# A new order of ScalarE's and GpSimd's steps in three feed-forward blocks, and rows of summed operands that begin at different places of a 256-byte line

## What is computed

```python
hn = rms_norm(h, norm2_g)                          # block 0
gate, up = jnp.split(hn @ w_gate_up, 2, axis=-1)
h = h + (jax.nn.silu(gate) * up) @ w_down
...
x = x + 0.5 * swiglu(rms_norm_2(x, ffn1_norm), ...)   # block 1, on the normalised end of the first model
...
x = x + 0.5 * swiglu(rms_norm_2(x, ffn2_norm), ...)   # block 2
```

## Time and profile before

| | us |
|---|---|
| median of 3 runs | 2016.6 |
| profiled execution | 2016.8 |
| its span, first to last instruction | 2015.0 |
| TensorE busy with matmuls | 1962.6 |
| GpSimd, VectorE, ScalarE busy | 1123.3, 1189.4, 937.5 |
| mean granted clock of TensorE | 0.99 |

### The profile page before, as it was taken

The page is one execution under the profiler, slowest core; times in us unless marked ns, Lnnn a source line. Parts: engine busy times, 40 slices in busy tenths (PEclk is TensorE's granted clock), DMA queues, the critical chain, the costliest instruction groups (busy, mean ns, idle before and its releaser), DMA issues.

```text
span 2015.0 us, 30682 instructions
## 1 busy us (share of the span) xinstructions
PE 1962.6 (97%) x11449; PEld 1731.6 (86%) x11449; DVE 1189.4 (59%) x2067; ACT 937.5 (47%) x1649; POOL 1123.3 (56%) x915
## 2 busy tenths in 40 slices
PE   9999999999899999979999999999999989999999
PEld 8998887888689989758898988889888878998987
DVE  6587656545446455765654655676645554646564
ACT  6413235534436435444462644667544453644532
POOL 4445452254567657546666766656555455765753
PEclk9999999999899999989999999999999989999999
DMA  5232321123233333322433333342222323333332
GB/s 181 83 102 87 102 86 51 55 84 105 66 102 106 105 88 102 98 70 79 111 105 100 92 103 105 85 110 78 83 87 84 105 74 94 106 105 97 97 111 84
DMA packets 253850, 189.68 MB, mean 94 GB/s; under 512 B 6608, under 2 KB 249680, under 8 KB 253680
## 3 DMA queue, kind: packets, MB, share of 16 engines
q1 hardware_dynamic: 253024, 187.53, 31.1%
q10 hardware_dynamic: 688, 0.31, 0.1%
HBM read 180.93 MB, written 2.10 MB: 91 GB/s over the span
## 4 chain that ended last, share of the span: by engine, by line
PE 86%; DVE 4%; POOL 4%; ACT 4%; issue 2%; DMA 0%; SPq 0%; DVEq 0%; ACTq 0%
PE ps L793 18%; PE ps L794 18%; PE ps L795 18%; PE ps L944 8%; PE ps L946 8%; PE ps L945 8%; POOL wlo L631 4%; PE ps L1133 1%; PE ps L1285 1%; ACT whi L1350 1%; DVE ps L1892 1%; PE ps L1205 1%; PE ps L1206 1%; PE ps L1207 1%; DVE tmp L1892 1%
## 5 line engine op out<-in xcount | busy, mean ns | idle before, releaser
L631 POOL TENSOR_TENSOR wlo<-raw,whi 128x512 fp32r<-128x512 f32 (+2 forms) x420 | 537.5, 1312 | 579.1 <-ACT whi L1350 433.9
L793 PE MATMUL ps<-xh,whi 128*128 128x512 f32 (+1 forms) x1008 | 383.5, 380 | 31.7 <-POOL wlo L631 31.7
L794 PE MATMUL ps<-xl,whi 128*128 128x512 f32 (+1 forms) x1008 | 375.2, 372 | 0.0
L795 PE MATMUL ps<-xh,wlo 128*128 128x512 f32 (+1 forms) x1008 | 375.1, 372 | 0.0
L1350 ACT ACTIVATE whi<-raw 128x2048 fp32r<-128x2048 f32 (+1 forms) x86 | 160.5, 1867 | 323.7 <-PE ps L795 279.2
L654 POOL TENSOR_TENSOR wlo<-raw,whi 128x512 fp32r<-128x512 f32 x162 | 212.9, 1316 | 160.1 <-ACT whi L1404 160.1
L793 PEld LDWEIGHTS ps<-xh,whi 128*128 128x128 f32 x1008 | 191.2, 190 | 65.0 <-POOL wlo L631 33.8
L795 PEld LDWEIGHTS ps<-xh,wlo 128*128 128x128 f32 x1008 | 190.8, 189 | 33.7
L793 PE MATMUL ps<-fh,whi 128*128 128x512 f32 x528 | 207.9, 394 | 9.2 <-POOL wlo L631 9.2
L794 PEld LDWEIGHTS ps<-xl,whi 128*128 128x128 f32 x1008 | 191.5, 190 | 28.9 <-issue 0.7
L794 PE MATMUL ps<-fl,whi 128*128 128x512 f32 x528 | 206.3, 391 | 0.0
(11 more groups left out here) (386 smaller groups left out, 4991.4 us busy)
## 6 DMA issues: line engine op xcount, KB each, us to landing
raw<-in_w_in SPq DMA_DIRECT2D x87, 512.0 KB, 4.6
raw<-in_w_gate_up SPq DMA_DIRECT2D x44, 512.0 KB, 5.1
raw<-in_ffn_w_gate SPq DMA_DIRECT2D x44, 512.0 KB, 4.0
raw<-in_ffn_w_up SPq DMA_DIRECT2D x44, 512.0 KB, 5.2
raw<-in_ffn_w_down SPq DMA_DIRECT2D x32, 512.0 KB, 4.5
raw<-in_w_down SPq DMA_DIRECT2D x16, 512.0 KB, 4.5
raw<-in_ffn_w_down SPq DMA_DIRECT2D x16, 384.0 KB, 3.8
raw<-in_w_b SPq DMA_DIRECT2D x8, 512.0 KB, 4.0
```

The source lines that it names most:

```text
L631: ins = pool.tensor_tensor(wlo[:, c % 2, cs], raw[:, c % 2, cs], whi[:, c % 2, cs].bitcast(F32), ALU.subtract)
L793: pe.matmul(o, w_of(whi), xhi, start=first, stop=False)
L794: pe.matmul(o, w_of(whi), xlo, start=False, stop=False)
L795: return pe.matmul(o, w_of(wlo), xhi, start=False, stop=last)
```

## The change

`FORMS_AT` gets a table of its own for block 1 (no quarter sums at place 0, two each at places 1 and 2). On ScalarE the quarter sums move from the front of a place to its end, Silu always stands behind `coming(0)`, the split of a down chunk behind a folded one is made two pieces at a time, `sum_high(4, 0)` moves from step 1 to step 2, and each feed of the third stage moves one tile back, the last one behind the first split of what follows. On GpSimd `act_low` comes behind `low` at places 7 and 19. On VectorE the eight multiplications of `hT` are made tile by tile in the four down chunks of the first stage. `down_chunk` waits for both accumulators of a folded chunk at once. In SBUF the four forms of the quarter sums and the six rows (two slots of three units) of the weight sums get 8 elements (32 bytes) more each, so that they begin at different places of a line (forms: 0, 32, 64, 96 bytes on; `fsl` 128 more; `foldh` 0 to 160, `foldl` 192 more, all from byte 128), and what stands behind them moves by up to 256 elements.

```diff
-FORMS_AT = {0: (0,), 1: (1, 2), 2: (3,)}
+FORMS_AT = ({0: (0,), 1: (1, 2), 2: (3,)}, {1: (0, 1), 2: (2, 3)})
...
-        fsh = at("fsh", 0, [P, 4, 4, FOLD], F32R)
-        fsl = at("fsl", 4096, [P, 4, 4, FOLD], F32R)
-        fh = at("fh", 8192, [P, RING, T], F32R)
-        fl = at("fl", 12800, [P, RING, T], F32R)
-        foldh = at("foldh", 17408, [P, 2, 3, 4 * P], F32R)
-        foldl = at("foldl", 20480, [P, 2, 3, 4 * P], F32R)
-        tmp = at("tmp", 23552, [P, 4, T])
...
+        fsh = at("fsh", 0, [P, 4, 4 * FOLD + 8], F32R)[:, :, 0:4 * FOLD].rearrange("p n (k t) -> p n k t", k=4)
+        fsl = at("fsl", 4128, [P, 4, 4 * FOLD + 8], F32R)[:, :, 0:4 * FOLD].rearrange("p n (k t) -> p n k t", k=4)
+        fh = at("fh", 8320, [P, RING, T], F32R)
+        fl = at("fl", 12928, [P, RING, T], F32R)
+        foldh = at("foldh", 17536, [P, 6, 4 * P + 8], F32R)[:, :, 0:4 * P].rearrange("p (s u) n -> p s u n", s=2)
+        foldl = at("foldl", 20656, [P, 6, 4 * P + 8], F32R)[:, :, 0:4 * P].rearrange("p (s u) n -> p s u n", s=2)
+        tmp = at("tmp", 23808, [P, 4, T])
...
@@ GpSimd, ffn
-                    if down_part(p) is not None and up_tile(p - 1) is not None:
+                    if down_part(p) == (2, 0):
                         act_low(f, p - 1)
                     if p + 1 < FFN_LEN:
                         low(C_F[f] + p + 1)
-                    if down_part(p) is None and up_tile(p - 1) is not None:
+                    if down_part(p) != (2, 0) and up_tile(p - 1) is not None:
                         act_low(f, p - 1)
@@ TensorE, down_chunk
-                    pe.wait_ge(acc_free, 2 * (c - 2) + t + 1)
+                    pe.wait_ge(acc_free, 2 * (c - 2) + (2 if folded(p - 2) else t + 1))
@@ ScalarE, fold_high
                 elif z == 1:
                     corner_high(1, 1, 1)
+                elif z == 2:
                     sum_high(4, 0)
-                elif z == 2:
                     sum_high(5, 1)
@@ ScalarE, ffn
-                        elif folded(p):
-                            high_piece(c + 1, z)
-                        elif p and z == 0:
+                        elif folded(p) and z < 2:
+                            high_piece(c + 1, 2 * z)
+                            high_piece(c + 1, 2 * z + 1)
+                        elif p and z == 0 and not folded(p):
                             high(c + 1)
...
-                    if n is not None and not folded(p - 1):
-                        act.wait_ge(acc_free, 2 * (c - 1) + 1)
-                        act.activation(tmp[:, 1, :], tmp[:, 0, :], ACT.Silu).then_inc(silu_done, 1)
-                    for i in FORMS_AT.get(p, ()):
-                        fold_forms(f, i, own)
                     coming(0)
-                    if folded(p - 1):
-                        act.wait_ge(acc_free, 2 * c)
+                    if n is not None:
+                        act.wait_ge(acc_free, 2 * c if folded(p - 1) else 2 * c - 1)
                         act.activation(tmp[:, 1, :], tmp[:, 0, :], ACT.Silu).then_inc(silu_done, 1)
...
                     coming(3)
+                    for i in FORMS_AT[f == 1].get(p, ()):
+                        fold_forms(f, i, own)
                     if down_part(p) is not None and down_part(p)[0] == 2:
-                        for t in range(2):
-                            m = 2 * down_part(p)[1] + t
+                        for m in range(max(2 * down_part(p)[1] - 1, 0), 2 * down_part(p)[1] + 1):
                             act.wait_ge(h_new, 3 * DK * f + 2 * DK + m + 1)
                             feed(S + 1, m, gain)
                 high(C_F[f] + FFN_LEN + 1)
+                act.wait_ge(h_new, 3 * DK * (f + 1))
+                feed(S + 1, DK - 1, gain)
@@ VectorE, ffn
-                    for i in FORMS_AT.get(p, ()):
+                    for i in FORMS_AT[f == 1].get(p, ()):
                         fold_sums(f, i, own)
...
-                    if f == 1 and (r, j) == (0, 0):
-                        for n in range(DK):
-                            x = hT[:, n, META:TM]
-                            stt(x, x, vec[:, V_FIN + n:V_FIN + n + 1], ssum[:, META:TM], ALU.mult, ALU.mult).then_inc(xn_done, 1)
-                        dve.wait_ge(xn_done, DK)
...
                         x = hT[:, m, META:TM]
+                        if f == 1 and r == 0:
+                            stt(x, x, vec[:, V_FIN + m:V_FIN + m + 1], ssum[:, META:TM], ALU.mult, ALU.mult).then_inc(xn_done, 1)
+                            dve.wait_ge(xn_done, m + 1)
                         done(c, t)
```

More of the change, by code:

```diff
@@ L208, in at @@
             return nc.alloc_sbuf_tensor_at(name, shape, dt, offset=start + 4 * off)
-        fsh = at("fsh", 0, [P, 4, 4, FOLD], F32R)
-        fsl = at("fsl", 4096, [P, 4, 4, FOLD], F32R)
-        fh = at("fh", 8192, [P, RING, T], F32R)
-        fl = at("fl", 12800, [P, RING, T], F32R)
-        foldh = at("foldh", 17408, [P, 2, 3, 4 * P], F32R)
-        foldl = at("foldl", 20480, [P, 2, 3, 4 * P], F32R)
-        tmp = at("tmp", 23552, [P, 4, T])
[L218 to L221, removed]
+        fsh = at("fsh", 0, [P, 4, 4 * FOLD + 8], F32R)[:, :, 0:4 * FOLD].rearrange("p n (k t) -> p n k t", k=4)
[5 more added lines that the diff above has]
+        tmp = at("tmp", 23808, [P, 4, T])
+        low_sum = at("low_sum", 25856, [P, 4, P])
+        prod1 = at("prod1", 26368, [P, FOLD])
+        prod5 = at("prod5", 26624, [P, FOLD])
+        prod6 = at("prod6", 26880, [P, FOLD])
         gt = at("gt", 22528, [P, 4, T])
```

## The result

The changed kernel takes **1966.4 us** (median of 4 runs, 1965.45 to 1967.49) against 2016.9 for the kernel before beside it (2016.38 to 2017.62): ratio 0.975, 95% interval 0.9733 to 0.9767, 50.5 us less. The profiled execution took 1966.0 us, its span is 1964.2, and the mean granted clock is 1.00, where it was 0.99.

A forecast was written before the change was run, and what follows sets the result against it. TensorE, busy 97%, was taken as the bound, so only its waits and matmul pace could give time. Order 52.6 us and places 2.4 made 55.0 off 2016.8, less 0.2: 1961.6 us; 8-in-10 range 1948 to 1975.

The forecast's parts named there:

- the order: All parts of the change except the SBUF rows; claimed to save 52.6 us in sum, mostly TensorE's waits.
- the places: Quarter chunks: operands of five of seven products begin elsewhere in a line; −7.8 to +2.9 us, middle taken, −2.4 us.
- Quarter sums behind the weights: Start of each feed-forward block: TensorE's long waits for `wlo` and the low clock after them go, 37.4 us gained.
- the sign of being wrong: Listed as showing the prediction wrong: a new wait at the fourth or fifth chunk of a block; no size given.
- the rival with 0.15: Block starts: the moved sums become the wait, three times 1 to 5 us, giving 1965 to 1977 us; chance 0.15.
- GpSimd's order and the multiplications: First down chunks of three blocks: `low` before `act_low` and `hT` multiplications spread out end TensorE's waits, 7.4 us gained.
- `sum_high(4)`: First quarter chunks of stages 1 and 2: `prod5` copied on time; `prod` waits of 6.1 us become 3.5, 2.6 gained.
- Two pieces at a time: First down chunk: `wlo` some 2 us earlier ends the wait at place 19, three times, 1.9 us; nothing at place 30.
- Feeds one tile later: Stage 2, block 0: three waits, 3.7 us, go; sums at block 1's start may be held 0.4; gain 3.3 us.
- that places cost, 0.2: Quarter chunks: the different starting places do nothing or cost, giving 1964 to 1967 us; chance 0.2.
- that they give half of 13 ns everywhere, 0.1: Quarter chunks: starting places give more; all 13 ns would be 42 us, 1922; half gives 1943 us; chance 0.1.
- Slower: Quarter chunks: every stream beginning off the line's grid pays 27 ns more, 87 us in all, giving 2051 us; chance 0.02.

## Why the prediction was right, and where it was not

1961.6 was forecast and 1966.4 came; faster, and within 1948 to 1975. Both halves were mis-sized, in opposite directions: the order gave 44.8 us for 52.6, the places 5.8 for 2.4. That the total is off by 5 us and the order alone by 8 is luck: the second error took back a part of the first.

- **Quarter sums behind the weights**, 37.4 forecast, 35.9 by its own run. The mechanism is as described: the split ahead of the `fsh` copies, waits and low clock gone. The cover was counted too well. At block 0's third chunk 0.98 us are lost for 0.6 forecast. Block 1 has none at its third, but 1.25 at its fourth, where the prediction had a cover of 0.3 (887.0 against 887.3) and counted nothing; the lengthened `rs` multiplication, 1.04 us, is not in that count. Block 2 has none. So the sign of being wrong, a new wait at the fourth or fifth chunk, did show once, and the rival with 0.15 came true in one block of three, at the small end of its 1 to 3 us.
- **GpSimd's order and the multiplications**, 7.4: the waits went as forecast, though no run has this part alone. The run of the sums alone still has the three waits at place 7, with the clock at 0.57 in block 1; the changed kernel has none.
- **`sum_high(4)`**, 2.6 forecast. The waits for `prod` stayed, at the fifth product, largest in block 1, as written: 0.26 idle in block 0's first, 2.41 in block 1. That 2.2 of the latter belong to the multiplications at place 10 is shown by their own run. But what stays is 4.8 us with restarts, where I had 3.5, so 1.3 less was gained.
- **Two pieces at a time**, 1.9: the wait at place 19 is gone three times, and at place 30 `fl` took its place, as forecast, but with 0.54 idle each where 0.36 had been.
- **Feeds one tile later**, 3.3: this step failed. The three waits of block 0's end are gone, 3.7 us. But the sentence that the chunks after blocks 1 and 2 have the last `xl` in time looked at the wrong consumer: TensorE's sums of squares (L910) come before it and want `ssl`, which stands behind the same feed. They wait 1.3 idle each time, and `ssum` and `tmp` another 1.0 at the start of block 1, where I had 0.4. And I had priced the delay at the length of the split alone. The split also starts GpSimd, and beside it the VectorE instructions of the chain took 1.4 to 1.8 us instead of 0.4 to 0.7. Its own run puts all this at 4.1 us; I had 0.4. Half of what the order fell short by is here.
- **The places**, 2.4, taken as the middle of −7.8 and +2.9. It was the middle for want of a row: the true 5.8 lies inside. The Trainium skill (SBUF — State Buffer, "Who interferes with whom") says that TensorE waits for no other engine and has two independent read ports. It says nothing there of where an operand begins; that the places would then give nothing was my reading of it, and the runs decide against that reading, with 5.1 us alone and 5.8 with the order.
- **The rivals**: that places cost, 0.2, is out; that they give half of 13 ns everywhere, 0.1, is out for the change, though two of seven products came to 113.5 ns in one layout. "Slower" is out: the quarter chunks ran at 118.66 ns in the mean, not above 120. With the weights half a line off, matmuls of 512 columns did lose pace, but 6 ns and not 27.

What the failed step lacked was the price of VectorE beside GpSimd, which the prediction had for the multiplications alone. The Trainium skill (SBUF — State Buffer, "Who interferes with whom") says that a VectorE instruction with two SBUF inputs contends with a GpSimd one that reads SBUF. The trace agrees with it: the two sums `ssum` and `ssl` took 1.77 and 1.65 us beside GpSimd's `wlo`, and 0.69 each without it.

## What to carry to other kernels

When a step is moved behind another on one engine, follow what that other step sets going: here the split freed GpSimd, whose work nearly tripled the time of three VectorE instructions between the late feed and TensorE. For each result that comes later, list all its consumers in the order in which the bound engine meets them, since the first of them decides, and that need not be the one that the result is made for. And where the cover is thin, ask what the moved step does to the pace of the engines beside it: a cover of 0.3 us was smaller than the 1.04 us by which one VectorE instruction grew. Where operands are laid out by hand, try a few common shifts and time the whole kernel, as one shift sped 256-column matmuls up and another slowed the 512-column ones.

## What the runs showed of the hardware

- The pace of a matmul changed with where its operands, and others, begin in a line: 256 columns ran at means of 113.5 to 120.0 ns for a product, 512 columns at 226.7 (same place), 228.8 (64 bytes apart) and 233.0 (128 apart). A line of 256 bytes is how the kernel counts places; no run tests whether the pace repeats after 256.
- It isn't a property of one pair of operands: `fsh` at byte 192 by `whi` at 128 took 113.3 ns with the weight sums at 192 and 117.9 with them at 128.
- Beside GpSimd's `wlo` a VectorE sum of 512 columns with two SBUF inputs took 1.65 to 1.78 us, without it 0.69; a cast took 1.40 and 0.43.
- The clock was granted at 1.00 behind TensorE's waits of 0.7 to 1.3 us and behind the one of 2.41 in block 1 (951.9 to 957.9), and at 0.57 over 4 us behind one of 2.83 in the run of the quarter sums alone.
